# State copies and compression weights issued in the delta stage, compression biases folded into the products, and three loads of a trunk reissued

## The reference

```
def _compress(x, pe, w):                 # x: (B, L, 2, 64), pe: (32, 64), w: (32, 64, 64)
    ch = x.reshape(B, n_chunk, 16, 2, 64)
    blocks = concatenate([ch[:, i:i + n_cmp] for i in range(2)], axis=2)   # 32 rows, stride 16
    blocks = blocks + pe[None, None, :, None, :]
    return einsum('bcjkd,jde->bcke', blocks, w)

mem_kv  = _mem_kv(mem_prompt, ...)       # 256 memory tokens: norm, two products, key norm
h = x + concatenate([o_nsa, o_gdn]) @ w_out
h = h + _cross_attn(h, mem_kv, ...)
h = h + _conv_ffn(h, ...)
# one of the outputs per sample: the last 512 rows of [cache_win, new rows]  ("win_s")
```

## Time and profile before

| | us |
|---|---|
| median of three runs | 3257.19 |
| lowest and highest | 3250.27, 3257.8 |
| the profiled execution | 3254.76 |
| its span, first to last instruction | 3253.1 |

### The profile page before, as it was taken

How to read it: one execution, slowest core, us unless ns; L and a number is a source line. 1 busy time by engine, 2 the same in 40 slices (tenths; PEclk the granted TensorE clock), 3 DMA queues, 4 the chain that set the end, 5 groups by cost and what they waited for, 6 DMA issues and landing times. The chain is left out here.

```text
span 3253.1 us, 36245 instructions
## 1 busy us (share of the span) xinstructions
PE 2810.9 (86%) x13550; PEld 1784.6 (55%) x13550; DVE 1141.0 (35%) x2417; ACT 671.0 (21%) x1153; POOL 509.1 (16%) x510
## 2 busy tenths in 40 slices
PE   8999967787546789658867999789999999999999
PEld 5555546776435344325543556556666666666665
DVE  3655545554223566224430000320434343430000
ACT  3344321111002456423321100211100000000000
POOL 0000002222001444333310300101100000000000
PEclk9999988888657899879988999999999999999999
DMA  5111110000141001488725320251111011102221
GB/s 185 43 43 43 43 33 14 13 6 13 42 101 35 23 20 46 127 264 265 249 100 194 125 93 0 104 186 71 47 39 38 26 39 39 39 15 52 66 66 39
DMA packets 230933, 242.64 MB, mean 75 GB/s; under 512 B 76306, under 2 KB 174099, under 8 KB 230675
## 3 DMA queue, kind: packets, MB, share of 16 engines
q1 hardware_dynamic: 209602, 163.19, 16.8%
q0 software_dynamic: 20112, 73.54, 6.5%
q10 hardware_dynamic: 1088, 4.20, 0.4%
HBM read 207.13 MB, written 37.94 MB: 75 GB/s over the span
## 5 line engine op out<-in xcount | busy, mean ns | idle before, releaser
L2947 PE MATMUL tr_acc<-tr_hnT,ahead_main 128*128 128x364 f32 (+1 forms) x2112 | 644.0, 468 | 0.0
L2947 PEld LDWEIGHTS tr_acc<-tr_hnT,ahead_main 128*128 128x128 f32 x2112 | 401.2, 190 | 242.1
L909 PE MATMUL front_wide<-front_w_nat,front_x 128*128 128x512 f32 (+1 forms) x576 | 224.2, 546 | 0.0
L909 PEld LDWEIGHTS front_wide<-front_w_nat,front_x 128*128 128x128 f32 x576 | 109.4, 190 | 107.5 <-issue 95.7
L2987 PE MATMUL tr_acc<-tr_early,tr_hnT 128*128 128x364 f32 (+1 forms) x528 | 161.5, 468 | 0.0
L2987 PE MATMUL tr_acc<-tr_early,ahead_main 128*128 128x364 f32 (+1 forms) x528 | 161.5, 468 | 0.0
L3312 DVE TENSOR_TENSOR tr_small<-tr_acc,tr_rbc 128x728 f32<-128x728 f32 x44 | 40.3, 916 | 337.6 <-PE tr_acc L2947 337.6
L895 PE MATMUL front_acc<-front_x,front_w_c 128*128 128x364 f32 (+1 forms) x480 | 150.5, 473 | 0.0
L2753 POOL TENSOR_TENSOR tr_early<-tr_small 128x1088 f32 x22 | 54.6, 2482 | 591.8 <-ACT tr_small L3133 591.8
L3133 ACT ACTIVATE tr_small<-tr_small 128x1088 f32<-128x1088 f32 x22 | 24.4, 1110 | 581.5 <-DVEq L3329 581.5
L2987 PEld LDWEIGHTS tr_acc<-tr_early,ahead_main 128*128 128x128 f32 x528 | 100.3, 190 | 60.6
(11 more groups left out here) (543 smaller groups left out, 4067.7 us busy)
## 6 DMA issues: line engine op xcount, KB each, us to landing
ahead_main<-in_cache_kv SPq DMA_DIRECT2D x136, 256.0 KB, 4.0
ahead_main<-in_w_up SPq DMA_DIRECT2D x44, 512.0 KB, 4.5
ahead_main<-in_cache_kv POOLq DMA_DIRECT2D x80, 256.0 KB, 4.8
ns_last<-in_cache_kv POOLq DMA_DIRECT2D x40, 256.0 KB, 4.6
tr_early<-in_cache_memT POOLq DMA_DIRECT2D x2, 4096.0 KB, 15.9
ahead_main<-in_cache_memV POOLq DMA_DIRECT2D x2, 4096.0 KB, 13.4
front_w_c<-in_w_chan SPq DMA_DIRECT2D x12, 512.0 KB
front_w_nat<-in_w_nat POOLq DMA_DIRECT2D x3, 2048.0 KB, 15.2
```

The costliest lines, as they stand in the source:

```text
L909: mm = pe.matmul(wide[:, s, 0:b - a], x[:, k, i * P:(i + 1) * P], w_nat[:, k, a:b], start=(k == 0), stop=(k == KD - 1))
L2947: mm = pe.matmul(acc[a][:, g, 0:hi - lo], w_up[:, n, a, k, :], hnT[:, k, lo:hi], start=(k == 0), stop=(k == KD - 1))
```

## The change

- SP's block of the prompt's delta stage gets 17 more transfers ahead of its loop: the whole `wblk` (now laid out on the host, 4 MB, one transfer) and the sixteen `win_s` copies.
- The keys stage has no weight load, no clearing, and eight row slots: four pairs of transfers, two tiles each, 384 columns of `rows`. `cT` is laid out by 16-row phase, with the position terms as two more columns, so that column 64 of each product is the bias. Two sets of 32 products stand in place of four, and one more small product spreads the value bias.
- In the samples' attention ACT issues the four constants and `wab` (one transfer, laid out on the host) where it issued the copies.
- In the trunk `mixT` is ACT's first instruction, `mem_w` is loaded in the stage before, and DVE waits for the four other constants only after the scaling.

```
 stage_delta_prompt, SP
                 sp.dma_start(gates[:, :, :], scr["misc"]...).then_inc(here, 16)
+                sp.dma_start(keys.wblk[:, :, :, :], io["cmp_wblk"]).then_inc(keys.w_here, 16)
+                for b in range(NB):
+                    sp.dma_start(io["win_s"][b, 0:WIN - NT, :], io["cache_win"][b, NT:WIN, :]).then_inc(keys.copied, 16)
+                    sp.dma_start(io["win_s"][b, WIN - NT:WIN, :], io["wrows"][...]).then_inc(keys.copied, 16)
                 with sp.Fori(0, ROUNDS) as i:
 stage_prompt_keys, SP
-                load(0, 0); load(1, 1)
+                for n in range(4):
+                    r = slice(2 * n * P, 2 * (n + 1) * P)
+                    sp.dma_start(rows[:, 2 * n:2 * n + 2, :], io["rows"][r, 0:384]...).then_inc(here[n], 16)
+                    sp.dma_start(wk[:, 2 * n:2 * n + 2, :], io["wrows"][r, 0:P]...).then_inc(here[n], 16)
+                sp.dma_start(pe_in[:, :, :], io["cmp_peT"]).then_inc(pe_here, 16)
                 sp.dma_start(vs...)
                 sp.dma_start(vw...)
-                with sp.Fori(0, 3) as i: ... load(2 * i + s + 2, s)
-                        sp.dma_start(wblk[r, c, :, r], io["cmp_w"][c]...).then_inc(w_here, 16)
-                    sp.dma_start(peT[r, :, :], io["cmp_peT"]).then_inc(w_here, 16)
 stage_prompt_keys, DVE, its end
+                dve.wait_ge(summed, 1)
+                dve.tensor_copy(vraw[0:65, :], acc[1][0:65, 0:P]).then_inc(raw_ready, 1)
+                dve.wait_ge(summed, 2)
+                dve.tensor_copy(kbias[:, :], acc[0][:, 64:65])
+                dve.drain()
+                dve.tensor_scalar(kc[:, 0:63], acc[0][:, 0:63], kbias[:, 0:1], None, ALU.add)
                 dve.wait_ge(bias_done, 1)
+                dve.tensor_copy(vbias[:, :], wide[:, 0:P])
                 dve.drain()
+                dve.tensor_tensor(vc[0:63, :], vraw[0:63, :], vbias[0:63, :], ALU.add)
 stage_trunk
  SP   -                sp.dma_start(aT[:, 0:4, 0:SEQ], scr["mixT"]...).then_inc(att_here, 16)
  ACT  +                act.dma_start(aT[:, 0:4, 0:SEQ], scr["mixT"]...).then_inc(att_here, 16)
  DVE  -                dve.wait_ge(const_here, 80)
       -                dve.wait_ge(ahead.memT_here, 16)
       +                dve.wait_ge(ahead.memT_here, 32)
                         for k in range(KD): ... memT[:, k, :] * mem_w[:, k:k + 1]
       +                dve.wait_ge(const_here, 64)
                         dve.wait_ge(hr_ready, 1)
```

More of the change, by code:

```diff
@@ L373, in _, with stage_delta_prompt @@
                 dve.sem_inc(o_ready, 1)
-def stage_delta_prompt(nc, io, scr, gT, ident, half):
+def stage_delta_prompt(nc, io, scr, gT, ident, half, keys):
     H, L, C = 4, 6, 64
@@ L1163, in _ @@
-                pe.wait_ge(w_here, 96)
+                for t in range(NK):
+                    s = t % 2
+                    pe.wait_ge(here[t // 2], 32)
+                    if t >= 2:
+                        pe.wait_ge(taken, t - 1)
+                    for n in range(3):
+                        pe.transpose(turned[s][:, n * P:(n + 1) * P], rows[:, t, n * P:(n + 1) * P], ident[:, :])
+                    pe.transpose(turned[s][:, 3 * P:4 * P], wk[:, t, :], ident[:, :]).then_inc(turn_done, 1)
@@ L1164, in _ @@
+                pe.wait_ge(keys.w_here, 16)
+                pe.wait_ge(pe_ready, 1)
+                pe.wait_ge(taken, NK)
                 for j in range(32):
-                    pe.matmul(bias_k[:, 0:1], wblk[:, 0, j, :], peT[:, 0, j:j + 1], start=(j == 0), stop=(j == 31))
+                    a = j // 16
+                    mm = pe.matmul(acc[1][0:65, 0:P], cT[:, 1, j % 16, a:a + 65], wblk[:, 1, j, :], start=(j == 0), stop=(j == 31))
+                mm.then_inc(summed, 1)
                 for j in range(32):
-                    m = pe.matmul(bias_v[:, 0:P], peT[:, 1, j:j + 1].to_broadcast([P, P]), wblk[:, 1, j, :],
-                                  start=(j == 0), stop=(j == 31))
@@ L1169, in _ @@
-                m.then_inc(bias_done, 1)
-                pe.wait_ge(taken, 10)
-                for j in range(32):
-                    pe.matmul(acc[0][:, 0:63], wblk[:, 0, j, :], cT[:, 0, j:j + 16 * 62 + 1:16], start=(j == 0), stop=(j == 31))
-                for j in range(32):
-                    m = pe.matmul(acc[1][0:63, 0:P], cT[:, 1, j:j + 16 * 62 + 1:16], wblk[:, 1, j, :], start=(j == 0), stop=(j == 31))
-                m.then_inc(summed, 1)
+                    a = j // 16
+                    mm = pe.matmul(acc[0][:, 0:65], wblk[:, 0, j, :], cT[:, 0, j % 16, a:a + 65], start=(j == 0), stop=(j == 31))
@@ L1177, in _ @@
+                mm.then_inc(summed, 1)
+                pe.wait_ge(raw_ready, 1)
+                pe.matmul(wide[:, 0:P], ident[0:65, 64:65].to_broadcast([65, P]), vraw[0:65, :], start=True, stop=True).then_inc(bias_done, 1)
             @block.scalar
             def _(act):
[L1179 to L1186 removed]
@@ L1188, in _ @@
-            @block.gpsimd
-            def _(pool):
-                pool.memset(wblk[0:HD, :, :, HD:P], 0.0).then_inc(cleared, 1)
+                for t in range(NK):
+                    act.wait_ge(turn_done, t + 1)
+                    act.activation(cT[:, :, :, 8 * t:8 * t + 8].rearrange("p c j n -> p c n j"),
+                                   turned[t % 2][:, 0:2 * P].rearrange("p (c n j) -> p c n j", c=2, j=16), ACT.Copy)
+                    act.activation(ks[:, t * P:(t + 1) * P], turned[t % 2][:, 2 * P:3 * P], ACT.Copy)
+                    act.activation(kw[:, t * P + WIN:(t + 1) * P + WIN], turned[t % 2][:, 3 * P:4 * P], ACT.Copy).then_inc(taken, 1)
@@ L1778, in first_weights, with stage_nsa_prompt @@
         return self.main[:, 4096 * n:4096 * (n + 1)].rearrange("p (k n) -> p k n", k=KD)
-def stage_nsa_prompt(nc, io, scr, ident, kbias, vbias, ahead):
+def stage_nsa_prompt(nc, io, scr, ident, kbias, vbias, keys, front, after):
     with ExitStack() as ctx:
@@ L1787, in stage_nsa_prompt, with stage_nsa @@
         vs, vw, vc = sb("vs", [P, 8, P]), sb("vw", [P, 12, P]), sb("vc", [64, P])
-        with nc.sbuf_tensor("wblk", [P, 2, 32, P], F32) as wblk:
-            stage_prompt_keys(nc, io, scr, ident, wblk, kbias, vbias, ks, kw, kc, vs, vw, vc)
+        stage_prompt_keys(nc, io, scr, ident, keys, kbias, vbias, ks, kw, kc, vs, vw, vc)
+        front.close()
+        ahead = Ahead(nc, after)
         stage_nsa_prompt_attend(nc, io, scr, ident, ks, kw, kc, vs, vw, vc, ahead)
-def stage_nsa(nc, io, scr, ident, half, ahead):
+    return ahead
+def stage_nsa(nc, io, scr, ident, half, keys, front, after):
     with ExitStack() as ctx:
@@ L1983, in _ @@
                 sp.dma_start(ahead.memT(), io["memT"].rearrange("(k p) n -> p k n", p=P)).then_inc(ahead.memT_here, 16)
+                sp.dma_start(ahead.mem_w[:, :], io["mem_norm_wT"]).then_inc(ahead.memT_here, 16)
                 for n in range(2):
@@ L2435, in stage_trunk @@
         small = st.sb("small", [P, 5 * TOK])
-        mem_w = st.sb("mem_w", [P, KD])
+        mem_w = ahead.mem_w
         att_w = st.sb("att_w", [P, KD])
@@ L3360, in _ @@
                 dve.memset(half[:, :], -0.5)
-        stage_channels_and_delta(nc, io, scr, ident, half)
-        ahead = Ahead(nc, ctx)
-        stage_nsa(nc, io, scr, ident, half, ahead)
+        front, after = ExitStack(), ctx.enter_context(ExitStack())
+        keys = stage_channels_and_delta(nc, io, scr, ident, half, front)
+        ahead = stage_nsa(nc, io, scr, ident, half, keys, front, after)
         stage_trunk(nc, io, scr, ident, half, ahead)
```

129 lines of the change are left out of this document (52 added, 77 removed).

## The result

The changed kernel takes 3176.77 us (median of 4 runs, 3171.59 to 3181.61) against 3257.11 for the kernel before beside it: a ratio of 0.9758 (95% interval 0.9734 to 0.9781), 80.3 us less. The forecast was 3168, 87 us less. The profiled executions differ by 73.1 us (spans 3253.1 and 3180.0), because that of after is the longest of its four runs.

| us | before | after | difference | forecast |
|---|---|---|---|---|
| prompt delta stage | 355.1 | 357.8 | +2.7 | 0 |
| keys stage | 74.4 | 30.2 | -44.2 | -41.5 |
| prompt's attention | 354.2 | 357.3 | +3.1 | 0 |
| samples' attention | 354.6 | 337.3 | -17.2 | -22.5 |
| trunk | 1547.6 | 1530.1 | -17.4 | -23.3 |

A forecast was written before the change was run, and what follows sets the result against it. TensorE does most of the work, so its waits in each stage were priced: 41.5 + 0 + 22.5 + 23.3 = 87.3 us less than the profiled 3254.76 gives 3167.5, forecast as 3168, range 3154 to 3186.

The forecast's parts named there:

- Part 1: Keys stage: bias products and the wait for weights go, its last work ends at 951.6; 41.5 us less.
- products at 14.5 + 3.05: Keys stage: 64 products take 14.5 us at full clock plus 3.05 for a slow start after idling, taken as 17.5.
- Rival A: Keys stage: the 64 products run at half clock throughout, 27.6 us in place of 17.5; total 3178, chance 0.12.
- Part 2: Prompt delta stage: the added 4 MB of weights and 4 MB of copies cost 0, bounds 0 to 3 us.
- Masks and gates were issued earlier on the same queue: Prompt delta stage: a reason given for putting the added transfers' cost at 0.
- Rival E: Delta stage: the queue moves so slowly that zt is late, making the kernel slower than before; 3279, chance 0.02.
- Part 3: Samples' attention: SP's pages no longer stand behind constants and weights, 21.0, plus 1.5 from window keys; 22.5 us less.
- Rival B: Samples' attention: pages become the bound and 9.1 us are given back; total 3177, chance 0.12.
- Part 4: Trunk: PE starts 8.7 us earlier and the output projection no longer waits for mixT; 23.3 us less, bounds 10 and 25.
- the 1 us set aside for `w_xv`: Trunk: 1 us allowed for the second half of the memory weights landing near 1741, when PE needs it near 1739.5.
- If PE no longer idles there, the 3.05 us of the slow start go too: Trunk, output projection: without the wait for mixT its first 48 passes lose their slow start, 3.05 us.
- Rival C: Trunk's start: mixT takes its whole 15.49 us from w_out, delaying root and weights; total 3181, chance 0.10.

The follow-up runs named there:

- Weights_late: Changed kernel with wblk loaded in the keys stage, as one transfer behind the row loads, folding kept; 3185.0 us.
- wab_behind: Changed kernel with wab still one transfer, but issued by SP behind the first pair's window keys instead of by ACT at the stage's start; 3168.1 us.
- wab_pieces: Changed kernel with wab back on SP as eight transfers in 64-float pieces behind the window keys; 3176.8 us.
- no_gap: Changed kernel with the ten mix tiles turned earlier, two after some of the memory products, so none is left behind the last product; 3172.1 us.
- copies_back: Changed kernel with the sixteen win_s copies back on ACT in the samples' attention, weights still in the delta stage; 3182.8 us.
- after_again: The changed kernel measured once more, without any edit; 3173.9 us.
- combined: Changed kernel with the edits of wab_behind, burst_after_gates and no_gap, and PE's first memory product waiting for DVE's scaling slice by slice; 3167.7 us.
- burst_after_gates: Changed kernel with SP waiting in the delta stage for masks, norm weight and gates to land before issuing wblk and the copies; 3172.5 us.
- mixT_back: Changed kernel with mixT back on SP's queue behind the ten mix tiles; 3183.7 us.
- bias_products: Changed kernel with the 64 bias products put back before the two sets of products in the keys stage, results unused; 3194.7 us.

## Why the prediction was right, and where it was not

**Part 1, right in mechanism, too careful by one term.** The step "products at 14.5 + 3.05" failed in its second number. The 3.05 came from a row where PE had idled for 15 us; here transposes run up to the products and 14.43 us were measured. Weights_late, with 6.06 us of idling, loses 1.98. Products began 14.1 us into the stage (13.6 forecast). Rival A fell.

**Part 2, not 0 but 2.7.** "Masks and gates were issued earlier on the same queue" was taken to mean that they land undisturbed. That was the step that failed, but not through the gates' own delay: it is 1.2 us in after and 0.1 in wab_behind, with the same growth. What the kernels with the burst share is a slower PE run (L560) and a later rise of the clock; the three that hold the burst back are shorter, and the link between burst and clock stays open. The bound of 3 held, and no engine waited for `zt`: the first one landed near 491, where the prediction had 530. Rival E fell.

**Part 3, right in sign, wrong in its reason.** The term of 22.5 measured 17.2. The step that failed is the reading of the 26.57 us as the price of the eight issues: wab_pieces shows 9.85. Taking the copies away alone brings 18.7 of the 19.2 us by which step 3's scores came earlier (52.7 to 34.0), taking the pieces away alone 13.0: the two work only together, and either edit would have won most of it. The same reading made me expect 1.5 us from the window keys, where the single transfer of `wab`, moved to the head, cost 1.1. That is 2.6 of the 5.3 us that are missing; 0.7 is in the pages of step 3 (19.2 in place of 22.5 in all at that point), and 2.0 went in the rest of the stage, whose length lies between 332.8 and 337.5 in the eight profiles that have its code unchanged; after's 337.3 is among the longest, so these 2.0 can be scatter. Rival B fell: from step 3's scores to the last ones ahead of the second compression it is 31.2 us, and 30.6 before.

**Part 4, right in mechanism, short by 5.9.** PE's start came 8.0 us earlier (8.7 forecast; DVE's scaling took 2.85 and not 2.20). From there to the last mix tile's copy it is 64.9 us and not 63.9. That is the 1 us set aside for `w_xv`, though in after it went in the first two products (16.73 us); where these took 15.4 to 15.6, PE waited 1.3 to 2.0 us for `w_xv`. The step that failed is "If PE no longer idles there, the 3.05 us of the slow start go too": PE has only a few short transposes to do in 4.5 us, since the last tile waits for a slot, and 17.44 was measured. Without that gap (no_gap) the slow start goes; but copies_back and weights_late have the gap and no slow start, so part of these 2.6 us is how after's execution fell. Some 2.5 us went in the cross-attention, where two runs of products (L2849, L2876) take 6.27 and 6.33 us that took 4.58 and 5.38 before; in after_again they take 4.58 and 5.38 again, so this is scatter. Rival C's delay of `w_out` came (5 us); of the 13 us that it was to cost, after shows none and four other profiles 1.3 to 2.0.

The Trainium skill's page DMA: Bandwidth & Descriptors (Issuing engines are not separate DMA queues) says that transfers of all issuers share the 16 engines. The trace agrees (`mem` 5.4 to 11.1 us, `w_out` 18.2 to 23.3 with `mixT` beside them), and it bears more weight than I gave it: SP's window keys were slowed by ACT's `wab`. What it says of the gain of issuing elsewhere did not decide here, since `mixT` had stood behind semaphores.

**The sum.** 2.7 - 44.2 + 3.1 - 17.2 - 17.4 is 73.0 us less, and with rests under 0.1 gives the 73.1 us of the spans. The median moved 7.2 us more, 4.8 for the long profiled run of after and 2.4 for the short one of before. That the forecast came within 9 us has some luck in it: by the spans it is 14.2 us off, and two misses of 2.7 us (keys and delta) cancel. 3176.8 is also what rivals A and B give (3178, 3177), but neither happened: both sets of products ran at full clock, and the pages gave back at most 0.6 us (31.2 against 30.6).

## What to carry to other kernels

An issue that takes long on a queue says that something is in front of it, perhaps another engine's transfers, and not what the instruction costs: before pricing it, look at what else is in flight. Small loads that are needed at a stage's start should have landed, or at least stand alone, before megabytes are issued by anyone. After each gain at a stage's start ask for the next late release on every engine that feeds it; here the root behind POOL's drain took back much of what two earlier starts had won (no_gap, combined). And before a difference between two profiles is explained, look for the same stage in kernels that share its code: here a second profile of the same kernel, or one with another edit, undid several readings.

## What the runs showed of the hardware

- The time that SP's queue spends on an issue depends on what is in flight, from its own queue or another's: eight pieces of `wab` 9.85 us, or 26.57 with the copies issued on ACT, and in weights_late `vw`'s issue, behind the 4 MB:

```profile
927.74 10.17 SPq L1153 DMA_DIRECT2D vw<-out_wrows  x1
```

  In after, with the same `vw` transfer and no weights ahead, it was 1.83 us.
- POOL's drain waits for transfers that POOL has issued: 10.63 us with `w_out` on POOL's queue, 0.25 without.
- The same instructions of the prompt's attention take 349.5 to 357.7 us, with the granted clock of one 40 us window between 0.54 and 0.76. In the delta stage the same PE run takes 1.95 us in before, burst_after_gates and combined, 2.44 in after and 3.11 in mixT_back, whose program up to there is that of after.
- In bias_products the clock fell from 1.00 to 0.50 at 936 under a PE that was busy throughout, with products of one column; it stayed there into the next run (0.54 between 945 and 950) and was at 1.00 for the two sets behind.
- The output projection's first 48 passes, behind the same gap of some 4.5 us, take 16.6 to 17.9 us in six profiles and 14.87 in two.
